# Encoder trunk on one core: the router of the last token tile in another order, without its filler products

## The reference

```python
x = x + jnp.concatenate([o_gla, o_fnet, o_mla], axis=-1) @ w_out[l]
x = x + hier_moe(rms_norm(x, norm2_g[l]), ...)

def hier_moe(h, ...):                       # 4 groups of 8 experts, D_EXPERT = 256
    grp_w, grp_idx = lax.top_k(softmax(t @ w_rg + b_rg), 1)
    in_grp = (t @ w_re + b_re) of the chosen group
    e_w, e_idx = lax.top_k(softmax(in_grp), 2)
    e_w = e_w / jnp.sum(e_w)
    for e in range(32):
        he = silu(t @ w_gate[e]) * (t @ w_up[e])
        y = y + combine[:, e:e + 1] * (he @ w_down[e])
return rms_norm(x, final_norm_g)
```

## Time and profile before

| | us |
|---|---|
| median of 3 runs | 533.57 |
| the runs | 531.96 to 536.53 |
| the profiled execution's own time | 531.99 |
| its span, first to last instruction | 530.2 |

### The profile page before, as it was taken

The page is one execution under the profiler, slowest core; times in us unless marked ns, Lnnn a source line. Parts: engine busy times, 40 slices in busy tenths (PEclk is TensorE's granted clock), DMA queues, the critical chain, the costliest instruction groups (busy, mean ns, idle before and its releaser), DMA issues.

```text
span 530.2 us, 7660 instructions
## 1 busy us (share of the span) xinstructions
PE 498.4 (94%) x2932; PEld 272.0 (51%) x2932; DVE 208.2 (39%) x546; ACT 137.3 (26%) x327; POOL 81.8 (15%) x101
## 2 busy tenths in 40 slices
PE   3999999999999999999999999999999996989785
PEld 3446544569755555445456555555555553444421
DVE  3217320663576770116773422222222222232166
ACT  4404211362476761203131111111111110102013
POOL 1000000344000000000213232222222222111000
PEclk9999999999999999999998999999999999989999
DMA  8996000010496004930089999999999999999984
GB/s 277 365 271 263 1 1 0 16 36 2 150 416 266 2 2 157 419 137 40 2 290 379 401 422 415 413 416 415 419 414 415 416 414 417 418 414 415 411 349 161
DMA packets 40422, 141.00 MB, mean 266 GB/s; under 512 B 9880, under 2 KB 13016, under 8 KB 32192
## 3 DMA queue, kind: packets, MB, share of 16 engines
q1 hardware_dynamic: 35472, 132.61, 64.0%
q0 software_dynamic: 4816, 7.85, 4.0%
q10 hardware_dynamic: 96, 0.03, 0.0%
HBM read 131.52 MB, written 16.39 MB: 279 GB/s over the span
## 4 chain that ended last, share of the span: by engine, by line
PE 73%; DMA 13%; SPq 6%; DVE 5%; issue 1%; ACT 1%; DVEq 0%; ACTq 0%; POOLq 0%
PE bank L1068 16%; PE bank L753 12%; PE bank L933 9%; PE bank L1081 8%; DMA EW<-in_moe_w_up 4%; PE bank L916 4%; SPq L620 3%; PE bank L1041 3%; PE bank L979 3%; DMA EW<-y_scratch 3%; PE bank L968 2%; DMA x_scratch<-X 2%; SPq L625 2%; PE bank L850 2%; DMA EW<-in_w_in 2%; PE bank L889 1%
## 5 line engine op out<-in xcount | busy, mean ns | idle before, releaser
L1068 PE MATMUL bank<-EW,WO 128*64 128x256 f32 x640 | 76.6, 394 | 8.1 <-DMA EW<-in_moe_w_up 6.9
L753 PE MATMUL bank<-EW,XT 128*128 128x512 f32 (+1 forms) x192 | 64.1, 495 | 0.0
L1068 PEld LDWEIGHTS bank<-EW,WO 128*64 128x64 f32 x640 | 46.3, 141 | 33.5 <-DMA EW<-in_moe_w_up 9.2
L1986 POOL DMA_INDIRECT y_scratch<-G,sidx x30 | 35.9, 1197 | 153.6 <-DVE G L1774 141.3
L933 PE MATMUL bank<-WO,XT 128*128 128x512 f32 x128 | 56.6, 595 | 0.0
L1396 ACT ACTIVATE G<-bank 128x128 f32<-128x128 f32 x32 | 8.9, 277 | 177.9 <-PE bank L1068 177.9
L753 PEld LDWEIGHTS bank<-EW,XT 128*128 128x128 f32 x192 | 32.9, 190 | 31.0 <-issue 31.0
L1761 DVE TENSOR_TENSOR G<-G,bank 128x128 f32<-128x128 f32 x32 | 9.2, 288 | 99.5 <-ACT G L1396 99.5
L1774 DVE COPY G<-bank 128x512 f32<-128x512 f32 x32 | 22.1, 692 | 61.6 <-PE bank L1081 61.6
L1081 PE MATMUL bank<-EW,G 128*64 128x512 f32 x160 | 38.7, 604 | 0.4 <-issue 0.4
L933 PEld LDWEIGHTS bank<-WO,XT 128*128 128x128 f32 x128 | 23.7, 190 | 27.3 <-issue 27.3
(11 more groups left out here) (288 smaller groups left out, 622.9 us busy)
## 6 DMA issues: line engine op xcount, KB each, us to landing
EW<-in_moe_w_gate SPq DMA_DIRECT2D x20, 1024.0 KB, 21.1
EW<-in_moe_w_up SPq DMA_DIRECT2D x20, 1024.0 KB, 21.2
EW<-in_moe_w_down SPq DMA_DIRECT2D x20, 1024.0 KB, 23.2
y_scratch<-MIX SPq DMA_DIRECT2D x8, 512.0 KB, 9.1
WO<-in_w_out SPq DMA_DIRECT2D x2, 2048.0 KB, 12.0
MIX<-in_moe_w_gate SPq DMA_DIRECT2D x4, 1024.0 KB, 18.8
MIX<-in_moe_w_up SPq DMA_DIRECT2D x4, 1024.0 KB, 20.0
WO<-in_moe_w_gate SPq DMA_DIRECT2D x4, 1024.0 KB, 19.1
```

Of the source, the lines that this page charges most:

```text
L753: mm = pe.matmul(ps[:, 0:width], xnT[:, c, t * P:(t + 1) * P], w_in_sb[:, c, col:col + width], start=(c == 0), stop=(c == C - 1))
L1068: mm = pe.matmul(bank[BLOCK * m:BLOCK * (m + 1), 0:2 * P].rearrange("p (w n) -> p w n", w=2), xeT[:, buf, c, par * BLOCK:(par + 1) * BLOCK ...
L1986: pool.indirect_dma_start(y_rows, bass.IndirectOffsetOnAxis(ap=sidx[:, col:col + 1], axis=0), Y[:, e % 2], None, bounds_check=4 * S - 1, o ...
```

## The change

Four things are changed, all in the router. In `OUT_ORDER` the step `("pick", 0)` goes from ahead of `("Lf", 3)` to behind `("L", 3)`, `("norm", 3)` goes ahead of `("Lf", 3)`, and `("pos", 3)` goes ahead of `("pick", 2)`. The `keep_busy` products are taken out. DVE's work on step `("pos", t)` is split in three functions (`positions`, `list_rows`, `list_places`), and for tile 2 the second, the third and `weights` are done later: `list_rows(2)` between the mean square of tile 3 and its refinement, `list_places(2)` after it, `weights(2)` after tile 3's choice. Lines of before.py are those of the profile.

```diff
--- before.py
+++ after.py
@@ -163,8 +163,8 @@
 
 OUT_ORDER = [("out", 0, 0), ("out", 0, 1), ("out", 1, 0), ("T", 0), ("norm", 0), ("out", 1, 1), ("Lf", 0),
              ("out", 2, 0), ("L", 0), ("T", 1), ("norm", 1), ("out", 2, 1), ("Lf", 1), ("pos", 0), ("T", 2), ("norm", 2),
-             ("L", 1), ("out", 3, 0), ("pos", 1), ("Lf", 2), ("L", 2), ("out", 3, 1), ("pos", 2), ("T", 3), ("pick", 0),
-             ("Lf", 3), ("norm", 3), ("L", 3), ("pick", 1), ("pick", 2), ("pos", 3), ("pick", 3)]
+             ("L", 1), ("out", 3, 0), ("pos", 1), ("Lf", 2), ("L", 2), ("out", 3, 1), ("pos", 2), ("T", 3), ("norm", 3),
+             ("Lf", 3), ("L", 3), ("pick", 0), ("pick", 1), ("pos", 3), ("pick", 2), ("pick", 3)]
 
 
 def attention_order():
@@ -734,10 +734,6 @@
                     if t == T - 1:
                         close_bank(mm, ("xT", c))
 
-            def keep_busy(ps, data):
-
-                pe.matmul(ps[:, :], ident[:, :], data, start=True, stop=True)
-
             def by_feature(key, col, width):
 
                 ps = open_bank(key)
@@ -1012,8 +1008,6 @@
                     ps = open_bank(step)
                     close_bank(pe.matmul(ps[:, 0:NG + NE], lf[t % 2], small[:, STACK:ONE_UP], start=True, stop=True), step)
                 elif kind == "pick":
-                    if t == T - 1:
-                        keep_busy(open_bank(("ids", 1)), X[:, 0, 0:512])
                     pe.wait_ge(sel_ready, 2 * t + 2)
                     drained(pe, ("out", t, 0))
                     drained(pe, ("out", t, 1))
@@ -1027,8 +1021,6 @@
                         mm.then_inc(pick_done, 1)
                 elif kind == "pos":
                     ps = open_bank(step)
-                    if t == T - 1:
-                        keep_busy(ps, X[:, 0, 0:512])
                     pe.wait_ge(picks_ready, t + 1)
                     for u in range(t + 1):
                         mm = pe.matmul(ps[:, 0:NE], tri[:, 1 if u < t else 0, :], mska[:, u, :],
@@ -1666,6 +1658,28 @@
                 link(dve.reciprocal(wts[:, t, 0:1], sc[:, 8:9]))
                 return dve.tensor_tensor(wts[:, t, 1:2], wts[:, t, 0:1], sc[:, 4:5], ALU.mult)
 
+            def positions(t, ps):
+                link(dve.scalar_tensor_tensor(pos1[:, t], ps[:, 0:NE], 1.0, mska[:, t], ALU.add, ALU.mult))
+                for e in range(2):
+                    dve.tensor_scalar(sel0[:, t, e], slot_no[:, e], pos1[:, t, e:e + 1], rn2[:, t, 2:3],
+                                      ALU.is_equal, ALU.mult).then_inc(sel_ready, 1)
+                dve.tensor_tensor(sel4[:, t].rearrange("p (a u) s -> p a u s", u=2),
+                                  pos1[:, t, 2:6].rearrange("p (a u) -> p a u", u=2).unsqueeze(3).to_broadcast([P, 2, 2, BLOCK]),
+                                  slot_no.unsqueeze(1).to_broadcast([P, 2, 2, BLOCK]),
+                                  ALU.is_equal).then_inc(sel4_ready, 1)
+
+            def list_rows(t, ps):
+                step = ("pos", t)
+                row, rows2 = rt[:, t, 10], rt[:, t, 11:13]
+                free_bank(dve.tensor_tensor(row, ps[:, 0:NE], small[:, 0:NE], ALU.add), step)
+                drained(dve, step)
+                link(dve.tensor_tensor(rows2, oh[:, t], row.unsqueeze(1).to_broadcast([P, 2, NE]), ALU.mult))
+
+            def list_places(t):
+                link(dve.tensor_reduce(rt[:, t, 0, 10:12], rt[:, t, 11:13], AX, ALU.add))
+                dve.scalar_tensor_tensor(dest[:, t, :], rt[:, t, 0, 10:12], -1.0, rt[:, t, 0, 10:12],
+                                         ALU.mult, ALU.max).then_inc(dest_ready, 1)
+
             for step in OUT_ORDER:
                 kind, t = step[0:2]
                 if kind == "out":
@@ -1680,8 +1694,12 @@
                     dve.tensor_scalar(rn2[:, t, 1:2], rn2[:, t, 0:1], rn2[:, t, 4:5], EPS, ALU.add, ALU.add).then_inc(var_ready, 1)
                     norms[0] += 1
                     dve.wait_ge(var_ready, norms[0])
+                    if t == T - 1:
+                        list_rows(t - 1, banks[PLAN[("pos", t - 1)][0]])
                     refine(rn2[:, t, 2:3], rn2[:, t, 1:2], rn2[:, t, 3:4])
                     dve.tensor_copy(lrow[:, t, :, 1], rn2[:, t, 2:3].to_broadcast([P, 2])).then_inc(row_ready, 1)
+                    if t == T - 1:
+                        list_places(t - 1)
                 elif kind == "T":
                     if t == T - 1:
                         ps = filled(dve, ("x2T", t, 1))
@@ -1705,26 +1723,16 @@
                     link(first_max(l32, NE, t, 9, oh[:, t, 1], sc[:, 7:8]))
                     dve.tensor_tensor(mska[:, t], oh[:, t, 0], oh[:, t, 1], ALU.add).then_inc(picks_ready, 1)
                     dve.tensor_tensor(sc[:, 5:6], sc[:, 7:8], sc[:, 6:7], ALU.subtract).then_inc(logit_ready, 1)
+                    if t == T - 1:
+                        link(weights(t - 1))
                 elif kind == "pos":
                     ps = filled(dve, step)
-                    link(dve.scalar_tensor_tensor(pos1[:, t], ps[:, 0:NE], 1.0, mska[:, t], ALU.add, ALU.mult))
-                    for e in range(2):
-                        dve.tensor_scalar(sel0[:, t, e], slot_no[:, e], pos1[:, t, e:e + 1], rn2[:, t, 2:3],
-                                          ALU.is_equal, ALU.mult).then_inc(sel_ready, 1)
-                    dve.tensor_tensor(sel4[:, t].rearrange("p (a u) s -> p a u s", u=2),
-                                      pos1[:, t, 2:6].rearrange("p (a u) -> p a u", u=2).unsqueeze(3).to_broadcast([P, 2, 2, BLOCK]),
-                                      slot_no.unsqueeze(1).to_broadcast([P, 2, 2, BLOCK]),
-                                      ALU.is_equal).then_inc(sel4_ready, 1)
-                    row, rows2 = rt[:, t, 10], rt[:, t, 11:13]
-                    free_bank(dve.tensor_tensor(row, ps[:, 0:NE], small[:, 0:NE], ALU.add), step)
-                    drained(dve, step)
-                    link(dve.tensor_tensor(rows2, oh[:, t], row.unsqueeze(1).to_broadcast([P, 2, NE]), ALU.mult))
-                    link(dve.tensor_reduce(rt[:, t, 0, 10:12], rows2, AX, ALU.add))
-                    dve.scalar_tensor_tensor(dest[:, t, :], rt[:, t, 0, 10:12], -1.0, rt[:, t, 0, 10:12],
-                                             ALU.mult, ALU.max).then_inc(dest_ready, 1)
-
-                    if t < T - 1:
-                        link(weights(t))
+                    positions(t, ps)
+                    if t != T - 2:
+                        list_rows(t, ps)
+                        list_places(t)
+                        if t < T - 1:
+                            link(weights(t))
             dve.wait_ge(pick_done, 1)
             dve.wait_ge(x2_stored, 16 * T)
             dve.tensor_copy(xg[0][:, 0:512], banks[0][:, :]).then_inc(picked, 1)
```

## The result

The changed kernel took 537.55 us (median, 534.81 to 540.08), the kernel before, run beside it, 533.31 us (531.63 to 536.53). The ratio is 1.0084, 95% interval 1.0069 to 1.0099: slower by 4.2 us or 0.8%, within 1% but above the range of the prediction. The profiled execution took 538.84 us, 6.9 more than that of before. All times are us.

What follows compares the result with a forecast made beforehand. The weight stream through the DMA engines was taken to set the end. The pick's 0.8 us gain was to stop at the store's wait, so the terms summed to 0: 533.5 us (median less 0.1), range 531.0 to 536.3 us.

Steps and rivals of the forecast that it cites:

- The logits 1.7 earlier, the last pick 0.8 earlier: Router's last tile: VectorE's logits read begins 1.7 us earlier, and the last pick gains 0.8 us.
- Removing the fillers costs nothing: Router: two fillers of 1.02 us lay in waits; removing them gives back at most part of the 0.8 us.
- The store sets when the tokens are copied, gain 0: Router's end: the copy of picked tokens waits for tile 3's store at 279.7 us, so gain 0.
- if these writes are the cause, the loss moves but stays; for the store I bound it by 0.8 us either way: Tile 2's list writes, some 2 us later: their 0.8 us loss only moves; store shift taken as 0.
- the dip to 259 GB/s: DMA stream, 2 us from 274 us behind tile 2's writes: 259 GB/s against 416, a loss of 0.8 us.
- 2.3 us of transfers are still queued, so expert 0 may end later by that much: Behind the router: expert 0 may end up to 2.3 us later before the DMA engines run dry.
- The stream sets the end: Expert stretch: the weight stream, DMA share 1.02 at 416 GB/s, sets the end; PE waits about 8 us.
- The page's rule of the clock: Store's wait: matmuls waiting for a DMA run cold; an earlier clock fall loses 1.4 us, held by queue, costing 0.
- the pick's gain arrives: Rival: PE, not the stream, sets the end; a router 0.8 us shorter gives 532.8 us; chance 0.14.
- the router runs at the lower clock: Rival: without fillers the clock falls from pick 0 through expert 0; +8.0 us, 541.6 us; chance 0.05.

Runs made afterwards that it cites:

- e1: Changed kernel with both keep_busy filler products put back ahead of the last tile's counts and pick; 537.95 us, ratio 1.0092.
- e2: Kernel before with only the two filler products taken out; 535.74 us, ratio 1.0051.
- h1: Kernel before without tile 2's two list writes, so part of the computation is missing; 531.19 us, ratio 0.9975.
- g1: Changed kernel without tile 2's two list writes, so part of the computation is missing; 530.06 us, ratio 0.9943.
- g2: Kernel before with one more GpSimd wait: tile 2's list writes held until tile 3's row copy; 536.52 us, ratio 1.0052.
- h4: Changed kernel with tile 2's list work, first and third picks and fillers put back; early root and tile 2's late weights kept; 532.05 us, ratio 0.9994.
- f2: e4 with one more GpSimd wait: tile 2's list writes held until tile 3's row copy; 537.67 us, ratio 1.0086.
- f4: e4 with SP issuing tile 3's store ahead of the three loads over w_out; 534.41 us, ratio 1.0027.
- h2: e4 with both filler products added back; 535.84 us, ratio 1.0057.
- e4: Changed kernel with tile 2's list work and weights back at their old place on VectorE; 533.92 us, ratio 1.0021.
- f3: Changed kernel with SP issuing tile 3's store ahead of the three loads over w_out; 533.91 us, ratio 1.0010.
- e3: Changed kernel with GpSimd holding tile 3's list writes until all four stores have landed; 536.49 us, ratio 1.0072.
- f1: Changed kernel with SP issuing expert 6's loads into XT only after the last tile's logits are taken; 536.68 us, ratio 1.0072.

## Why the prediction was wrong

- *The logits 1.7 earlier, the last pick 0.8 earlier*: right, both to 0.1.
- *Removing the fillers costs nothing*: right in the new order, where e1 gave nothing back. But e2 shows that they carried 2.7 us in the old order, which the prediction did not see.
- *The store sets when the tokens are copied, gain 0*: the gate was right, its time was not. The step that failed is the term "if these writes are the cause, the loss moves but stays; for the store I bound it by 0.8 us either way". The prediction saw that tile 2's writes come some 2 us later, and it sized what they can do by the dip to 259 GB/s. That dip is not theirs: h1, without them, has 254 GB/s there. And it took their loss to be the same at any place. The runs show one that depends on the place: the writes cost some 6 us more in the changed kernel than before (g1 against h1), and moving them alone from 2.5 to 6.5 behind the first load costs the kernel before about 3 us (g2). The store took 14.63, 2.2 more, against a bound of 0.8. The bound came from a single place and from a dip that was only assumed to be the writes', and no rival gave the moved writes a price of their own.
- *2.3 us of transfers are still queued, so expert 0 may end later by that much*: in its size it held, but not its premise that nothing else empties the queue. Expert 0's end moved by some 4.7 (26.89 - 22.2), so 2.4 were to be lost, and the stream lost 2.0 at 293 to 296. The hole at 279 to 283 took 2.8 more, and that one no queue could cover: requests were there, and the DMA engines did not get through them.
- *The stream sets the end*: right, and it is why the loss arrived in full: 1.6 MB or 3.9 us missing in 34 us, and the same 412 to 416 GB/s in both kernels behind it.
- *The page's rule of the clock*: the Trainium skill ("TensorE: Matmul & The Clock Gate", section "Loop structure matters more than you think") was drawn on for a fall at the store's wait. The trace agrees, and more so than before: after the wait of 3.22 the clock was at 0.51, and expert 0 took 6.58, 1.5 more than before. It is behind the hole, not its cause, as g2 shows at a clock of 1.00.
- *The rivals*: "the pick's gain arrives" was refuted here by the hole, g1 against h1 would give it 1.1 to 1.7 us where the writes are gone, but not clear of the noise, and in h4 a copy 0.8 earlier brought nothing that the interval shows; "the router runs at the lower clock" was wrong for this kernel, but such a fall came in e2, f2, f4 and h2; none was the mechanism that decided.

Shown is that the later issue of tile 2's list writes makes the hole (e4, g1, g2). That the store and the late expert 0 carried a part of it to the time is seen in f3 and in the trace, how large a part is open. How a write of 8 bytes does it is open as well. The Trainium skill ("DMA: Bandwidth & Descriptors", section "Issuing engines are not separate DMA queues") says that transfers of every issuing engine run on the same 16 DMA engines and interleave; the trace agrees, since the packets of GpSimd's writes stand among SP's. That alone does not say why the price depends on the place, and no run isolates it. The profiles do show what goes with it. In the seven kernels with the hole of slow 8 KB packets (the changed one, e1, e3, f1, f2, f3, g2) the last packet of tile 2's writes starts 0.3 to 3.8 us after the first 8 KB packet of the loads into XT. In the kernel before and in e2, e4, f4, h2 and h4 it starts 0.8 to 1.9 us ahead of it.

## What to carry to other kernels

A transfer that is moved must be priced at its new place in the queue, however few bytes it has, and where the trace knows only the old place, the loss seen there is one point of the range and not its end. Whether that loss is the transfer's own has to be tested first: here a run without the writes kept the dip. To take an instruction group "into a wait" of one engine is only free if nothing that it releases is a transfer: here four list instructions of some 0.2 us were hidden well and cost some 3 us (e4, g2) in the DMA queues. To find where time went in a kernel bound by its stream, align both traces at the first load and compare the bytes moved since, window by window: the first 34 us held 3.9 of the 5.6 us that the profiled executions differ by behind that load.
